# A hybrid decoder step on one Trainium2 core: the first inputs of the attention and GLA stage are loaded and prepared between the last gate units of the projection

## What is computed

```python
z = rms_norm(h, norm_w) @ w_in                       # 1024 -> 3600 columns
dq, dk, dv, dg, gq, gk, gv, gg, ga = split(z)        # attention q k v gate, GLA q k v gate, decay
lg = log_sigmoid(ga @ gla_wa2 + gla_ba) / 16         # decay per token and channel

# differential attention, per head, with a relative bias that is banded for the nearest 128 keys
a = softmax(q k^T * scale + bias)                    # two maps per head
o_d = (a[0] - lam * a[1]) @ v

# GLA, per chunk of 128 tokens
b = cumsum(lg)
A[t, s] = sum_d q[t,d] * exp(b[t,d] - b[s,d]) * k[s,d]      for s <= t
o_g = (q * exp(b)) @ S + A @ v
S   = exp(b_last) * S + (k * exp(b_last - b))^T @ v

out = h + concat(norm(o_d) * silu(dg), norm(o_g) * silu(gg)) @ w_out
```

## Time and profile before

| | us |
|---|---|
| median of 3 runs | 1117.42 |
| range of the runs | 1112.53 to 1118.14 |
| the profiled execution | 1116.9 |
| its span, first to last instruction | 1115.2 |
| busy: TensorE, VectorE, ScalarE, GpSimd | 933.9, 571.1, 464.2, 285.9 |
| mean granted clock of TensorE, as a share of full speed | 0.929 |

### The profile page before, as it was taken

One profiled execution on the slowest core, in us unless ns is written; L12 is line 12 of the kernel. 1 busy time (PEld: TensorE's weight loads), 2 busy tenths in 40 slices (PEclk: granted clock), 3 DMA queues, 4 the chain that ended last, 5 costly groups with the idle time before them and its releaser, 6 DMA issues. The chain is left out here.

```text
span 1115.2 us, 23837 instructions
## 1 busy us (share of the span) xinstructions
PE 933.9 (84%) x8297; PEld 733.6 (66%) x8297; DVE 571.1 (51%) x958; ACT 464.2 (42%) x1269; POOL 285.9 (26%) x438
## 2 busy tenths in 40 slices
PE   4899989888899998798987999157778788867998
PEld 4897789656576565466665779146667666646886
DVE  4767642544445343345544522477777768355221
ACT  4744443222222234323332434258767677344100
POOL 2010300232133222132222320485766523000000
PEclk9999989999999998899999999558898999968999
DMA  7457843697889788699989851742212111115221
GB/s 220 128 155 221 317 153 112 204 346 291 296 303 353 269 300 273 211 305 342 325 283 326 289 182 40 230 95 80 71 53 57 23 33 29 48 41 189 90 99 52
DMA packets 141492, 207.29 MB, mean 186 GB/s; under 512 B 23634, under 2 KB 85708, under 8 KB 141372
## 3 DMA queue, kind: packets, MB, share of 16 engines
q1 hardware_dynamic: 120476, 138.10, 38.2%
q0 software_dynamic: 20832, 67.60, 17.7%
q10 hardware_dynamic: 64, 0.07, 0.0%
HBM read 181.25 MB, written 24.45 MB: 184 GB/s over the span
## 5 line engine op out<-in xcount | busy, mean ns | idle before, releaser
L553 POOL DMA_DIRECT2D vraw<-in_cache_v x256 | 137.3, 536 | 519.8 <-PE po L919 443.7
L823 PE MATMUL pz<-wh,xTh 128*128 128x256 f32 (+1 forms) x576 | 175.7, 305 | 5.2 <-DVE wl L1014 5.2
L1097 DVE STREAM_TRANSPOSE kx<-kraw 128x2048 f32<-128x2048 f32 x64 | 147.6, 2307 | 44.3 <-DMA kraw<-in_cache_k 43.4
L823 PE MATMUL pz<-wh,xTl 128*128 128x256 f32 (+1 forms) x576 | 166.1, 288 | 0.0
L823 PE MATMUL pz<-wl,xTh 128*128 128x256 f32 (+1 forms) x576 | 165.8, 288 | 0.0
L823 PEld LDWEIGHTS pz<-wh,xTh 128*128 128x128 f32 (+1 forms) x576 | 109.2, 190 | 37.9 <-issue 23.1
L823 PEld LDWEIGHTS pz<-wh,xTl 128*128 128x128 f32 (+1 forms) x576 | 109.5, 190 | 0.0
L823 PEld LDWEIGHTS pz<-wl,xTh 128*128 128x128 f32 (+1 forms) x576 | 109.2, 190 | 0.0
L819 PE MATMUL pz<-xTh,wh 128*128 128x384 f32 (+1 forms) x288 | 100.9, 350 | 0.0
L819 PE MATMUL pz<-xTh,wl 128*128 128x384 f32 (+1 forms) x288 | 94.9, 330 | 0.0
L819 PE MATMUL pz<-xTl,wh 128*128 128x384 f32 (+1 forms) x288 | 94.8, 329 | 0.0
(11 more groups left out here) (238 smaller groups left out, 1761.8 us busy)
## 6 DMA issues: line engine op xcount, KB each, us to landing
kraw<-in_cache_k SPq DMA_DIRECT2D x256, 256.0 KB, 5.5
vraw<-in_cache_v POOLq DMA_DIRECT2D x256, 256.0 KB, 5.3
wraw<-in_w_in SPq DMA_DIRECT2D x112, 128.0 KB, 5.5
out<-nat SPq DMA_DIRECT2D x32, 128.0 KB, 3.4
spare<-in_w_out SPq DMA_DIRECT2D x8, 512.0 KB, 4.1
vraw<-in_x_prompt SPq DMA_DIRECT2D x7, 512.0 KB, 4.3
xr<-in_x_prompt SPq DMA_DIRECT2D x7, 512.0 KB, 3.7
out<-xr SPq DMA_DIRECT2D x7, 512.0 KB, 2.6
```

The costliest lines, as they stand in the source:

```text
L553: pool.dma_start(vraw[:, t % VR, n, :], page_rows(cache_v, page)).then_inc(v_in[t % VR], 16)
L823: ins = pe.matmul(z[0:r, 0:CB], a[:, k, P * x:P * x + r], b[:, w, :], start=(n == 0), stop=(n == 3 * KT - 1))
L1097: dve.transpose(kx[:, GRP * g:GRP * g + GRP, :].rearrange("p n x -> p (n x)"), kraw[:, t % KR, :, :].rearrange("p n x -> p (n x)")).then_i ...
```

## The change

The start of stage 2 is taken apart, and most of it goes into stage 1.

- Buffers are shared between the stages: `early` is `kraw` in stage 1 and then holds keys, queries, GLA's first inputs and the anti-diagonal; `spare` is `kx` and then the GLA factors; `wp` is `wraw` and then the bands, later the turned probabilities; `stg` and `qzb` are shared as well.
- The sync engine, in iteration NU - 10 of stage 1, waits for the last turned keys and for older stores, and issues ten loads for stage 2; in iteration NU - 5 it loads the bands.
- GpSimd, behind its last load of values, clears `dd` and makes the exponents of tile 0. ScalarE does tile 0's exponentials in iterations NU - 3 and NU - 2. VectorE clears `qzb` in NU - 6 and does tile 0's factors in NU - 1 and, behind the last gate, in NU.
- The sync engine no longer waits for the last stores of `stg` at the end of stage 1, but in stage 2, behind its loads of two value tiles, the mask, `vg` and the second keys, and ahead of `load_gg(0)`.
- The low part of the bands goes from VectorE to GpSimd, behind `split_lo(0)`.
- IN leaves the list of GLA steps, so the planner places the other 48 anew: A0, A1, KO, DS and MX of tile 0 stood in half units 2, 4, 6, 8 and 10 and stand in 0, 2, 4, 6 and 8.

The diff, cut to its core:

```diff
+        early = sb(ctx, "early", [P, 4096])
+        spare = sb(ctx, "spare", [P, 8192])
+        wp = sb(ctx, "wp", [P, 6 * CB])
+        stg = sb(ctx, "stg", [P, 3, 384])
+        qzb = sb(ctx, "qzb", [P, 1024])
+        ebl = sb(ctx, "ebl", [P, 2, 2, NB])
+
+        kst = early[:, 0:1024].rearrange("p (h t) -> p h t", h=H)
+        qst = early[:, 1024:2048].rearrange("p (a h t) -> p a h t", a=2, h=H)
+        gst = early[:, 2048:3584].rearrange("p (a n m t) -> p a n m t", a=2, n=3, m=2)
+        turnr = early[:, 3584:3584 + P]
+        band_raw = wp[:, 0:2 * H * P]
+        dd = spare[:, fsize:2 * fsize].rearrange("p (n a m t) -> p n a m t", n=NL, a=2, m=2)
+        f0 = spare[:, 2 * fsize:3 * fsize].rearrange("p (n a m t) -> p n a m t", n=NL, a=2, m=2)
+        qzg = qzb[:].rearrange("p (a h m t) -> p a h m t", a=2, h=2, m=2)
+        own = [slice(0, DK), slice(DK, P)]
...
+                    if u == NEXT_L:
+                        sp.wait_ge(kx_done, NG)
+                        for n in range(NSTG):
+                            sp.wait_ge(stg_out[n], 16 * len(range(n, FIRST_G, NSTG)))
+                        sp.dma_start(kst, kT_d[:, :, 0:2 * P]).then_inc(k_st, 16)
+                        for n, of in enumerate((gqT_d, gkT_d, bT_d)):
+                            sp.dma_start(gst[:, 0, n], of[:, :, 0:P]).then_inc(gst_in[0], 16)
+                        for i in range(2):
+                            sp.dma_start(qst[:, i], qT_d[:, :, P * i:P * i + P]).then_inc(q_st[i], 16)
+                        for n, of in enumerate((gqT_d, gkT_d, bT_d)):
+                            sp.dma_start(gst[:, 1, n], of[:, :, P:2 * P]).then_inc(gst_in[1], 16)
+                        sp.dma_start(turnr, c_anti).then_inc(band_in, 16)
+                    if u == NEXT_B:
+                        sp.wait_ge(wlo_done, NSL)
+                        shifted = bass.AP(tensor=band_d.tensor, offset=0, ap=[[1, P], [384, H], [1, 2 * P]])
+                        sp.dma_start(band_raw.rearrange("p (h x) -> p h x", h=H), shifted).then_inc(band_in, 16)
...
-                for n in range(NSTG):
-                    sp.wait_ge(stg_out[n], 16 * len(range(n, len(stages), NSTG)))
...
+                b = gst[:, 0, 2]
+                pool.wait_ge(sc_done, NCH)
+                pool.wait_ge(gst_in[0], 48)
+                linked(pool.memset(dd[:, 0:LV - 1], 0.0))
+                level_exponents(pool, linked, b)
+                pool.tensor_copy(dd[:, LV, 0], b)
+                pool.tensor_scalar(dd[:, LV - 1], dd[:, LV - 1], 80.0, None, ALU.min).then_inc(dexp_in, 1)
...
+                    if u == NU - 3:
+                        act.wait_ge(dexp_in, 1)
+                        act.wait_ge(sc_done, NCH)
+                        for n in range(0, 3):
+                            act.activation(f0[:, n], dd[:, n], ACT.Exp)
+                    if u == NU - 2:
+                        for n in range(3, NL):
+                            act.activation(f0[:, n], dd[:, n], ACT.Exp)
+                        act.activation(ebl[:, 0, :, 0:1], gst[:, 0, 2, :, P - 1:P], ACT.Exp).then_inc(dexp, 1)
...
+                    gq, gk = gst[:, 0, 0], gst[:, 0, 1]
+                    if u == NU - 6:
+                        dve.wait_ge(sc_done, NCH)
+                        dve.memset(qzb[:], 0.0).then_inc(dzero, 1)
+                    if u == NU - 1:
+                        dve.wait_ge(dexp, 1)
+                        dve.wait_ge(dzero, 1)
+                        for hh in range(2):
+                            dve.tensor_tensor(qzg[own[hh], 0, hh], f0[own[hh], LV, 0], gq[own[hh]], ALU.mult)
+                        dve.tensor_tensor(f0[:, 0:LV, 0], f0[:, 0:LV, 0], gq.unsqueeze(1).to_broadcast([P, LV, 2, P]), ALU.mult)
+                    if u == NU:
+                        dve.tensor_tensor(f0[:, :, 1], f0[:, :, 1], gk.unsqueeze(1).to_broadcast([P, NL, 2, P]), ALU.mult)\
+                           .then_inc(fdone, 1)
...
-            steps = [("IN", 0)]
+            steps = []
...
-                load_keys(0)
-                load_queries(0)
-                sp.dma_start(turnr, c_anti).then_inc(band_in, 16)
-                shifted = bass.AP(tensor=band_d.tensor, offset=0, ap=[[1, P], [384, H], [1, 2 * P]])
-                sp.dma_start(pT[:, 0:2 * H, :].rearrange("p (h a) x -> p h (a x)", a=2), shifted).then_inc(band_in, 16)
-                load_g(0)
-                load_queries(1)
                 load_values(0)
                 load_values(1)
-                load_g(1)
                 sp.dma_start(mask[:], c_mask).then_inc(mask_in, 16)
                 load_vg(0)
+                load_keys(1)
+                for n in range(NSTG):
+                    sp.wait_ge(stg_out[n], 16 * len(range(n, len(stages), NSTG)))
                 load_gg(0)
-                load_keys(1)
                 load_vg(1)
...
                 split_lo(0)
-                pool.memset(dd[:, 0:LV - 1], 0.0).then_inc(dd_clear, 1)
-                exponents(0)
+                pool.wait_ge(bandhi_done, 2)
+                pool.tensor_tensor(bands[:, 1], band_raw, bands[:, 0].bitcast(F32), ALU.subtract).then_inc(bandlo_done, 1)
...
-                act.wait_ge(eps_in, 1)
                 queries_hi(0)
                 keys_hi(0)
-                act.wait_ge(band_in, 16 * 2)
+                act.wait_ge(band_in, 32)
                 act.activation(turn_hi[:], turnr, ACT.Copy).then_inc(bandhi_done, 1)
-                act.activation(bands[:, 0], pT[:, 0:2 * H, :].rearrange("p j x -> p (j x)"),
-                               ACT.Copy).then_inc(bandhi_done, 1)
+                act.activation(bands[:, 0], band_raw, ACT.Copy).then_inc(bandhi_done, 1)
+                act.wait_ge(eps_in, 1)
...
-                dve.wait_ge(bandhi_done, 2)
-                dve.tensor_tensor(bands[:, 1], pT[:, 0:2 * H, :].rearrange("p j x -> p (j x)"),
-                                  bands[:, 0].bitcast(F32), ALU.subtract)\
-                   .then_inc(bandlo_done, 1)
                 dve.memset(mixT[:, H:2 * H, P * (TILES - 1) + TAIL:P * (TILES - 1) + S0], 0.0)
-                dve.memset(qz[:], 0.0).then_inc(dzero, 1)
-                dve.wait_ge(dzero, 1)
```

More of the change, by code:

```diff
@@ new lines, in hymba_kernel @@
+        turnr = early[:, 3584:3584 + P]
[4 more added lines that the diff above has]
+        own = [slice(0, DK), slice(DK, P)]
+        k_st = sem("k_st")
+        q_st = [sem(f"q_st{n}") for n in range(2)]
+        band_in = sem("band_in")
@@ new lines, in hymba_kernel, with level_exponents @@
+        gst_in = [sem(f"gst_in{n}") for n in range(2)]
+        bandhi_done = sem("bandhi_done")
+        bandlo_done = sem("bandlo_done")
+        qhi_done = sem("b_qhi_done")
+        qlo_done = sem("b_qlo_done")
+        dexp_in = sem("dexp_in")
+        dexp = sem("dexp")
+        fdone = sem("fdone")
+        dzero = sem("dzero")
+        def level_exponents(pool, linked, b):
+            v = lambda a: a.rearrange("p m (n x) -> p m n x", x=DIAG)
+            ref = v(b)[:, :, :, DIAG // 2 - 1:DIAG // 2].to_broadcast([P, 2, P // DIAG, DIAG])
+            pool.tensor_tensor(v(dd[:, LV - 1, 0]), v(b), ref, ALU.subtract)
+            linked(pool.tensor_tensor(v(dd[:, LV - 1, 1]), ref, v(b), ALU.subtract))
+            last = b[:, :, P - 1:P].to_broadcast([P, 2, P])
+            pool.tensor_tensor(dd[:, LV, 1], last, b, ALU.subtract)
+            for n, half in enumerate(HALVES):
+                v = lambda a: a.rearrange("p m (n two x) -> p m n two x", two=2, x=half)
+                nb = P // (2 * half)
+                to_q, to_k, bb = v(dd[:, n, 0]), v(dd[:, n, 1]), v(b)
+                if nb == 1:
+                    for m in range(2):
+                        ref = b[:, m, half - 1:half].to_broadcast([P, half])
+                        pool.tensor_tensor(dd[:, n, 0, m, half:P], b[:, m, half:P], ref, ALU.subtract)
+                        pool.tensor_tensor(dd[:, n, 1, m, 0:half], ref, b[:, m, 0:half], ALU.subtract)
+                    continue
+                ref = bb[:, :, :, 0, half - 1:half].to_broadcast([P, 2, nb, half])
+                pool.tensor_tensor(to_q[:, :, :, 1, :], bb[:, :, :, 1, :], ref, ALU.subtract)
+                pool.tensor_tensor(to_k[:, :, :, 0, :], ref, bb[:, :, :, 0, :], ALU.subtract)
@@ L123, in hymba_kernel @@
             pages = sb(st, "pages", [1, NB * NPAGES], I32)
-            kraw = sb(st, "kraw", [P, KR, GRP, W])
-            kx = sb(st, "kx", [P, CHP, W])
+            kraw = early[:].rearrange("p (a n x) -> p a n x", a=KR, n=GRP)
+            kx = spare[:].rearrange("p (n x) -> p n x", n=CHP)
             vraw = sb(st, "vraw", [P, VR, GRP, W])
@@ L362, in hymba_kernel @@
             stage_no = {x: n for n, x in enumerate(stages)}
+            FIRST_G = min(n for n, x in enumerate(stages) if x[0] == "g")
+            assert all(x[0] == "g" for x in stages[FIRST_G:])
+            NEXT_L, NEXT_B = NU - 10, NU - 5
             def stage_free(eng, n):
@@ L553, in _, with linked @@
```

(29 more changed lines are left out.)

74 lines of the change are left out of this document (17 added, 57 removed).

## The result

The changed kernel takes 1096.34 us (median of 4 runs, 1093.71 to 1099.42) where the kernel before took 1114.97 beside it (4 runs, 1106.85 to 1118.14): 0.9854 of the time, with a 95% interval from 0.9812 to 0.9896. Beside the first four experiments the kernel before has a median of 1111.91 (22 runs, 1102.94 to 1119.67). The forecast was 1104.9, the range ended at 1099: the gain was larger than the range held. The profiled execution took 1099.42, with a span of 1097.8 and a mean granted clock of 0.933.

The account below looks back on a forecast made before the run. TensorE was taken as the bound, with two gaps where stage 2 starts. From 1116.9 us, barrier, loads and turns gave 5.0, the second gap 6.2, unit 1 1.2, units 2 to 4 -0.4: 12.0, so 1104.9 us; range 1099 to 1112.

Parts of the forecast that it names:

- What bounds the kernel: Start of stage 2: TensorE idles 19.39 us before the first scores and 9.23 before the first turn; shifting this reaches the end.
- The barrier: End of stage 1: the 128x1280 product replaces the last store's landing, 702.4 against 702.8, gain 0.4 us.
- The cover at the end of the projection: End of stage 1: the inserted loads and GpSimd, ScalarE and VectorE work fit into idle time; nothing taken for the loads.
- The first gap: Before the first scores: loads' 5.3 us go, VectorE and GpSimd taking turns cost 0.7; TensorE starts 5.0 us earlier, barrier included.
- The second gap: Between first scores and first turns: unit 0's turn 11.2 us ahead, unit 1's 12.4, leaving 12.0 by the fifth turn.
- the next late one is GpSimd: Unit 1 of stage 2: GpSimd's tile 1 exponents, 7.2 us, end at 718.2; ScalarE comes to them at 720.5.
- From there both kernels do the same work: After the fifth turn: both kernels run alike, one GLA step apart, so the 12.0 us lead stays.
- The base of the sum: The sum starts from one profiled execution, 1116.9 us; the median of the runs, 1117.4, is half a microsecond more.
- Only the first gap lasts: Rival: the second gap's gain is given back in later units, with GpSimd late; 5.0 us gained, 1111.9; chance 0.13.
- More closes: Rival: GpSimd and VectorE do not meet (2.4 us), the missing step saves one or two later; 1101 us; chance 0.14.
- Does not do what it says: Rival: loads are early but stage 2's start waits for something as late, such as a store; 1117 us; chance 0.05.
- Slower, TensorE's clock: Rival: the new order of small units holds TensorE's clock low longer; 1129 us after 40 us more; chance 0.06.

Follow-up runs that it names:

- first four experiments: The follow-up runs e1 to e4, measured beside runs of the kernel before with a median of 1111.91 us.
- e3: The kernel before with only the early loads and the later wait for the last stores: 1104.31 us, 0.9936 of the kernel before.
- e4: The changed kernel with tile 0's exponentials and factors two units earlier and tile 1's exponents in stage 1: 1094.69 us, 0.9849 of the kernel before.
- e7: e4 with the low part of the bands back on VectorE: 1090.33 us, 0.9825 of the kernel before.
- e8: The changed kernel with the ten early loads issued twice, the second set after the first landed: 1095.85 us, 0.9890 of the kernel before.
- e1: The changed kernel again, no edit: 1096.37 us, 0.9862 of the kernel before.
- e11: e5 once more, no further edit: 1098.40 us, 0.9879 of the kernel before.
- e5: The changed kernel with the 48 GLA steps at the kernel before's half units, IN only taken out: 1095.97 us, 0.9860 of the kernel before.
- e12: e7 once more, no edit: 1091.75 us, 0.9819 of the kernel before.
- e10: e7 with the GLA steps at the half units of the kernel before: 1093.70 us, 0.9858 of the kernel before.
- e9: The kernel before with only the GLA steps of tiles 1 to 9 and last state at the changed kernel's half units: 1111.90 us, ratio 0.9999.
- e2: The changed kernel's buffers with every load, step and wait at the kernel before's place: 1111.22 us, 1.0000 of the kernel before.

## Why the prediction was right or wrong

**What bounds the kernel, right.** Both gaps closed as far as the prediction said, and the shift reached the end.

**The barrier, right.** 0.4 said; the sync queue's first DMA of stage 2 stands 4.37 us behind the last product against 4.86: 0.5. The 128x1280 product did take the place of the store's landing. What it costs there was not named: without it (e3, e4, e7) the queue goes on at 3.40.

**The cover at the end of the projection, right.** "I take nothing" for the ten loads holds: from the store before them to the last product 58.41 to 58.44 us pass in 13 of the 14 traces, with the loads and without, and 59.92 in e8 alone. Their issue took 9.7 us (636.34 to 646.03), not 6, and still the load of the weight slice behind them went out as far ahead of the last product as in before (44.21 us, 44.20). GpSimd's memset and exponents ran from 660.3 to 668.2, earlier than said.

**The first gap, right in sum.** 5.0 said, 5.14 measured. In turns: queries 3.4, bands 2.5, keys 2.8 were said, and 3.32, 2.57 and, with the bands, 4.83 came out, so bands and keys together took 0.5 less than their sum. The row of 2.80 held waits for GpSimd's exponents; with nothing beside them the keys steps take 2.45 (e7). The choice of turns over an overlap was the right one.

**The second gap, right in size, with one step wrong.** Turn of unit 0: 11.2 said, 11.42 measured. Unit 1: 12.4 said, 13.1 measured. The step "the next late one is GpSimd" fell: its exponents ended at 713.9, and ScalarE's exponentials began at 716.55, right behind ScalarE's own previous step; e4, with these exponents gone, was no faster there. The sum did not rest on it, since it had GpSimd done at 718.2 and ScalarE there only at 720.5. Fifth turn: 12.0 said, 12.4 measured. The bounds of this part were wider than its error.

**"From there both kernels do the same work", wrong by about 2.** The lead grew from 12.4 at the fifth turn to 14.5 at the output products, in e1 from 12.5 to 14.4, in e8 from 12.3 to 15.3. With the old places (e11) it stayed, 13.15 and 13.5. Execution against execution, the new places bring 0.9 to 4.7 us with the early tile 0 (the changed kernel, e1 and e8 against e5 and e11), 1.6 to 3.7 in e7 and e12 against e10, and nothing without it (e9). Why they pay only there was not settled: of one kernel's executions, e5 and e11 lie 2.9 apart and e7 and e12 2.1, so that hardly more than the sign is safe. Stage 3 gave some back: from the first output product to the end of the span before took 104.4 us and the changed kernel 105.1 (e1 too), which the sum had at nothing and no run was made for. It repeats (104.4 and 104.5 in e2 and e9, 105.1 in e8), yet e4, e5 and e11, with the early start too, have 104.2 or 104.3: its cause is open. Net of it the change is worth 13.8.

**The base of the sum, the step that put the time outside the range.** It was made against one execution of 1116.9 us, with "half a microsecond" to the median. Of the 14 profiled executions of this case, whichever kernel, that one has the latest end of the projection:

| | last product of the projection, us |
|---|---|
| kernels without the early loads | before 697.84, e2 690.99, e9 688.02 |
| kernels with them | 697.29, 694.26, 690.66, 689.50, 689.38, 688.97, 688.60, 687.63, 687.48, 685.92, 684.08 |

The scatter lies ahead of the change. The last 58.4 us of the projection, with the early loads or without, are the same in all traces but e8's, so all of the spread of 13.8 us stands in the part before, where no load of the change has yet been issued. These are executions of eleven kernels on several chips; of one and the same program the end differs by 5.7 us (the changed kernel and e1), 5.4 (e7 and e12) and 8.3 (e5 and e11). The three runs of before, 1112.53 to 1118.14, had 5.6 us of this in them, and the range had none. The miss of 8.5 us is made up so: 3.6 for the end of the projection in the two profiled executions (697.84 against 694.26), 1.8 for the gain (13.8 against 12.0), and 3.1 by which the median of the changed kernel's runs lies below its profiled execution (1099.42 against 1096.34). The same forecast from before's later median, 1111.91 - 12.0 = 1099.9, lies 3.6 above 1096.34. So 6.7 of the 8.5 us are chance that a range had to hold, and 1.8 lie in the terms: 0.4 more up to the fifth turn, 2.1 for "the same work, one GLA step apart", which was put at nothing, and 0.7 back in stage 3. What moves the first part of stage 1 was not tested. The early loads can't have shortened it, since it ends before they are issued; the new buffers did nothing that e2 can tell; and e3's ratio (0.9936, so 7.1 us with an interval from 3.9 to 10.3) asks for no more than its 6.7 in stage 2.

**The rivals.** "Only the first gap lasts" fell: 14.5 us of lead at the output products, not 5. "More closes" gave the nearest time, 1101, by luck, since its mechanism was wrong: VectorE and GpSimd do meet, and no step was saved in later units; the 2 us gained there came with the new places. "Does not do what it says" fell with the first scores. "Slower, TensorE's clock" fell: 0.63 where before had 0.50.

## What to carry to other kernels

Work taken across a stage's seam was worth here what the engines behind it had lost in waiting, and one trace priced it step by step to within 0.7 us at each of four marks; but take positions from the last instruction that both kernels share, not from the start of the span, and put the scatter of the shared part, which the spread of the runs shows, into the range. To ask whether inserted work has cover, measure from the last shared instruction ahead of it to the first behind it: that told a loss of 1.5 us in e8, which the ratio could not. The low part moved from VectorE to a free GpSimd was no gain here, because VectorE's neighbouring steps read two operands from SBUF: price such a move as turns. When a plan of small steps shifts by half a unit, compare ends, not the middle.

## What the runs showed of the hardware

Three things stand out. A GpSimd subtraction of 128x1024 takes 2.57 us, during which VectorE's two-operand steps stand still, against 1.23 for the same subtraction on a VectorE with nothing beside it, and a GpSimd step of 128x256 takes 1.62 beside such steps against 0.64 alone. The first stage ended up to 13.8 us apart over 14 executions, and up to 8.3 apart for one program (e5 and e11), but its last 58.4 us repeated to 0.03 us in all but e8; the following 300 us repeat to 0.15 us in some pairs (after and e1) and to no better than 2.9 in others (e5 and e11). And a fall of the granted clock (0.76 instead of 1.00 over 7 us) came at one place in three of ten traces, in e12 but not in e7, which is the same program, and went with a loss of about 1.2 us each time.
